# GpSimd's first two cache copies: 48 and 48 blocks on 16 engines become 24 and 72 blocks laid out eight wide

## What is computed

```python
def trunk_layer(x, start_pos, conv_buf, pool_buf, k_buf, v_buf, ...):
    h = rms_norm(x, norm_g)
    proj = jnp.einsum('btd,de->bte', h, w_in)
    ...
    kk = jnp.concatenate([k_buf, k], axis=1)
    vv = jnp.concatenate([v_buf, v], axis=1)
    o = dilated_attention(q, kk, vv, k_buf.shape[1])
    ...
    new_k = kk[:, -n_keep:]
    new_v = vv[:, -n_keep:]
    y = jnp.einsum('bte,ed->btd', jnp.concatenate([ya, yb, yc], axis=-1), w_out)
    return x + y, new_conv, new_pool, new_k, new_v
```

## Time and profile before

| | |
|---|---|
| median of 3 runs | 399.57 us (398.87 to 400.03) |
| profiled execution's own time | 398.96 us |
| span of its trace | 397.1 us |
| TensorE busy | 343.2 us (86%) |
| bytes moved by the 16 DMA engines | 157.73 MB, mean 397 GB/s |
| granted TensorE clock, mean | 0.946 |

### The profile page before, as it was taken

The page is one execution under the profiler, slowest core; times in us unless marked ns, Lnnn a source line. Parts: engine busy times, 40 slices in busy tenths (PEclk is TensorE's granted clock), DMA queues, the critical chain, the costliest instruction groups (busy, mean ns, idle before and its releaser), DMA issues.

```text
span 397.1 us, 4745 instructions
## 1 busy us (share of the span) xinstructions
PE 343.2 (86%) x1550; PEld 270.0 (68%) x1550; DVE 232.3 (58%) x530; ACT 100.1 (25%) x237; POOL 58.5 (15%) x110
## 2 busy tenths in 40 slices
PE   3897799998879859989958999999979867989990
PEld 2676578886557646578847888888747644658880
DVE  2603769759975996431013489978985997540110
ACT  4300013542523122411011011453352222230011
POOL 4007740003400011044001320000600002000000
PEclk9999989999969898999996999999978998989997
DMA  8999999999999999999999999999999999999982
GB/s 300 422 414 402 419 417 403 419 421 414 420 419 417 420 415 401 409 413 416 411 404 415 417 418 409 421 421 417 421 419 417 416 386 355 376 396 384 389 346 87
DMA packets 44329, 157.73 MB, mean 397 GB/s; under 512 B 6988, under 2 KB 20116, under 8 KB 44306
## 3 DMA queue, kind: packets, MB, share of 16 engines
q0 software_dynamic: 14624, 88.25, 54.5%
q10 hardware_dynamic: 14420, 41.52, 26.4%
q1 hardware_dynamic: 15262, 27.67, 18.7%
HBM read 140.23 MB, written 104.46 MB: 616 GB/s over the span
## 4 chain that ended last, share of the span: by engine, by line
PE 50%; DVE 14%; SPq 12%; DMA 10%; issue 5%; ACTq 4%; ACT 4%; DVEq 0%
PE pj L704 24%; PE pj L847 14%; SPq L491 11%; DMA kg<-in_cache_k_win 10%; DVE yc L1307 3%; PE psc L776 3%; PE ptr L622 3%; DVE ssc L1251 2%; ACTq L471 1%; PE ps L824 1%; ACTq L885 1%; DVE spsum_pad L1277 1%; DVE tok L1245 1%; DVE sc L1213 1%; PE ps L830 1%
## 5 line engine op out<-in xcount | busy, mean ns | idle before, releaser
L704 PE MATMUL pj<-hT,wt 128*128 128x264 f32 x800 | 195.5, 403 | 7.4 <-DVE hT L1162 5.0
L704 PEld LDWEIGHTS pj<-hT,wt 128*128 128x128 f32 x800 | 157.0, 200 | 39.7 <-issue 12.7
L1307 DVE SCALAR_TENSOR_TENSOR yc<-u_ext,par,yc 128x256 f32<-128x256 f32 x180 | 77.2, 480 | 3.8 <-DVE u_smp L1191 1.0
L847 PE MATMUL pj<-mix,wt 128*128 128x264 f32 x256 | 61.1, 395 | 0.0
L847 PEld LDWEIGHTS pj<-mix,wt 128*128 128x128 f32 x256 | 49.2, 195 | 8.4
L611 POOL DMA_DIRECT2D out<-in_cache_v_win x48 | 26.2, 553 | 143.3 <-issue 143.3
L1377 DVE TENSOR_TENSOR xT<-xT,pj 128x264 f32<-128x264 f32 x16 | 6.9, 430 | 55.2 <-PE pj L847 55.2
L611 POOL DMA_DIRECT2D out<-in_cache_k_win x48 | 26.4, 557 | 82.0 <-issue 82.0
L965 ACT ACTIVATE ex<-pj 128x264 f32<-128x264 f32 x22 | 8.6, 390 | 77.1 <-PE pj L704 44.0
L1245 DVE TENSOR_TENSOR tok<-kg,qb 128x1536 f32<-128x1536 f32 x10 | 17.6, 1758 | 4.2 <-DMA kg<-in_cache_k_win 3.7
L1189 DVE SCALAR_TENSOR_TENSOR u_ext<-ex,pj 128x256 f32<-128x256 f32 x6 | 2.5, 421 | 29.9 <-ACT ex L965 29.9
(11 more groups left out here) (187 smaller groups left out, 334.8 us busy)
## 6 DMA issues: line engine op xcount, KB each, us to landing
wt<-in_w_tiles ACTq DMA_DIRECT2D x62, 512.0 KB, 32.3
out<-in_cache_k_win POOLq DMA_DIRECT2D x24, 1080.0 KB, 44.4
out<-in_cache_v_win POOLq DMA_DIRECT2D x24, 1080.0 KB, 81.3
out<-in_cache_k_win POOLq DMA_DIRECT2D x8, 1200.0 KB, 72.0
out<-in_cache_v_win POOLq DMA_DIRECT2D x8, 1200.0 KB, 89.3
out<-in_cache_k_win POOLq DMA_DIRECT2D x16, 432.0 KB, 64.2
out<-in_cache_v_win POOLq DMA_DIRECT2D x16, 432.0 KB, 87.3
kg<-in_cache_k_win SPq DMA_DIRECT2D x32, 144.0 KB, 33.5
```

Source lines behind the costliest of these rows:

```text
L704: last = nc.tensor.matmul(pj[n % RING][:, 0:T], wt[:, g % WRING, k, :], hT[:, k, :], start=(k == 0), stop=(k == KD - 1))
L847: last = nc.tensor.matmul(pj[n % RING][:, 0:T], wt[:, g % WRING, k, :], mix[:, k, :], start=(k == 0), stop=(k == KD - 1))
L1307: last = V.scalar_tensor_tensor(out=yc[:, t, 0:SEQ], in0=x_w, scalar=par[:, ROW_CW + w * CT + t:ROW_CW + w * CT + t + 1], in1=yc[:, t, 0:S ...
```

## The change

In layer 1, kind "k", sample 0, the border between the first two copies moves from row 768 to row 384: 24 blocks and 72 blocks in place of 48 and 48. Line 605 lays these two out as 8 groups (of 3 and of 9 blocks) in place of 16 groups of 3. Rows, bytes, pieces, the number of copies, their order and their semaphores stay; every other copy is unchanged.

```diff
+HALVES_CUT = 8 * 3 * DEEP_STEP
+
+
+def engines_of(l, kind, s, a):
+
+    return 8 if (l, kind, s) == (DEPTH - 1, "k", 0) and a < FAR_LO else 16
+
+
+def main_zones(l, kind, s):
+
+    if engines_of(l, kind, s, 0) == 8:
+        return (0, HALVES_CUT), (HALVES_CUT, FAR_LO)
+    return ((0, FAR_LO // 2), (FAR_LO // 2, FAR_LO)) if (kind, l) in DEEP else ((0, EVEN_CUT), (EVEN_CUT, EVEN_ROWS))
+
+
 def copies_of(l):
 
     return [(kind, s, a, b) for kind in ("k", "v") for s in range(NS)
-            for a, b in (*(((0, FAR_LO // 2), (FAR_LO // 2, FAR_LO)) if (kind, l) in DEEP else ((0, EVEN_CUT), (EVEN_CUT, EVEN_ROWS))),
-                         (FAR_LO, GATHER[0][0]))]
+            for a, b in (*main_zones(l, kind, s), (FAR_LO, GATHER[0][0]))]
...
                     elif (kind, l) in DEEP:
-                        dst, src = (t.rearrange("(c e f) h d -> c e (f h d)", c=16, f=DEEP_STEP)[:, :, 0:(DEEP_STEP - 1) * C_ATT]
+                        dst, src = (t.rearrange("(c e f) h d -> c e (f h d)", c=engines_of(l, kind, s, a), f=DEEP_STEP)[:, :, 0:(DEEP_STEP - 1) * C_ATT]
                                     for t in (out[l, s, a:b], cache[l, s, a + 1:b + 1]))
```

## The result

The changed kernel took 400.7 us (median of 7 runs, 399.92 to 401.87), the one before 399.07 us (median of 7 in the same session, 398.06 to 400.03): ratio 1.0044, 95% interval 1.0025 to 1.0062, so 0.44% slower. Predicted were 401.3 us and +0.44%. The traced execution took 401.87 us, the longest of the seven and 1.2 us above their median; the traced one before took 398.96 us, close to its own. In what follows a block is one of 23,040 bytes, and a change of the time is always the ratio to the kernel before in the same session; 0.1% is 0.4 us.

A forecast was written before the change was run, and what follows sets the result against it. The prediction took one late DMA engine to bound the kernel: two more blocks at 0.89 us add 1.8 us, so 398.96 + 1.8 = 400.7 us for the profiled execution and 399.57 + 1.8 = 401.3 us (+0.44%) for a median; range 398.4 to 402.5.

The forecast's parts named there:

- The straggler bounds the kernel: At the end, one DMA engine works alone for the last 3.9 us to 396.2; its end plus 0.9 us is the span.
- the first eight: The eight engines on which an eight-row transfer lies; the engine that ends last was said to be one of them.
- Twelve engines: The 24 and 72 blocks each lie on twelve engines, giving eight engines 8 blocks instead of 6; chance 0.69.
- +1.8 us: Added time on the last-ending engine: two more blocks at 0.89 us each.
- Carried along to the end: The early delay stays in POOL's queue on the last-ending engine, which runs dry near 394 in place of 392.3.
- Weights and gathers not held back, computation unmoved: Engines take a packet of each queue in turn, so added packets delay only POOL's later copies, not weights and gathers.
- single-engine stretch: At the end, the DMA share falls to 0.06 at about the old time and stays there some 2 us longer.
- Same count of POOL packets: In the trace after, POOL's queue has the same number of packets and bytes as before.
- Eight engines a copy, in turn or the same eight: Rivals on the two copies: different eights, -1.3 us, chance 0.13; both on the same eight, +5.3 us, chance 0.04.
- Nothing shows: Rival: copies still dealt over about 16 engines, or the early backlog absorbed in idle time; 399.6 us, chance 0.11.
- The new wait in the middle: Rival: uneven POOL queue delays POOL's issue and state stores that layer 1's loads need; at most 1 us, no own chance.
- a lighter first eight: Small copy on the eight engines that include the last-ending one, 3 blocks instead of 6: 1.3 us gained, chance 0.13.

The follow-up runs named there:

- run 10: Kernel before with layer 1's first pair cut 40/56 in samples 0 and 1, each behind its own tiny two-piece POOL transfer: 398.75 us, ratio 0.9989.
- run 4: Kernel before with the first pair cut 40/56 behind a tiny POOL transfer of 8 rows of 256 B: 401.21 us, ratio 1.0050.
- run 1: Kernel before with the first pair (kind k, sample 0) cut into 40 and 56 blocks, no tiny transfer: 401.47 us, ratio 1.0051.
- run 12: Kernel before with only layer 1's last pair (kind v, sample 7) cut into 72 and 24 blocks: 394.91 us, ratio 0.9883.
- run 2: Kernel before with the first pair cut into 32 and 64 blocks, so every engine keeps 6: 399.64 us, ratio 1.0003.
- run 3: Kernel before with the kind k pairs of samples 0 and 1 cut 40/56, no tiny transfer: 401.02 us, ratio 1.0025.
- run 5: Kernel before with the first pair cut 40/56 behind a tiny POOL transfer of 8 rows of two 128 B pieces: 396.98 us, ratio 0.9949.
- run 7: Kernel before with samples 0 and 1 cut 40/56, the tiny POOL transfer ahead of the second pair: 403.6 us, ratio 1.0117.
- run 9: Kernel before with the first pair cut into 72 and 24 blocks behind the tiny POOL transfer: 396.11 us, ratio 0.9918.
- run 11: Kernel before with only layer 1's last pair (kind v, sample 7) cut into 40 and 56 blocks: 396.73 us, ratio 0.9931.
- run 6: Kernel before with 48 and 48 blocks kept and only the tiny POOL transfer added ahead of them: 399.17 us, ratio 1.0004.
- run 8: Kernel before with the first pair cut into 24 and 72 blocks behind the tiny POOL transfer: 400.03 us, ratio 1.0021.

## Why the prediction was right

**The straggler bounds the kernel: shown.** By the blocks on engines 4 to 6 against before: -4 gave 0.9918 and 0.9883 (and only 0.9989 in run 10, where the upper eight got 4 more), -2 gave 0.9949 and 0.9931, 0 gave 1.0003 and 1.0004, +2 gave 1.0044 and 1.0051 (and 1.0050 in run 4), +4 gave 1.0117. The time follows the blocks of a few engines, up and down, while the bytes in all are the same. Where the computation ends doesn't account for it: the spans of runs 1 and 12 are 7.0 us apart (400.1 and 393.1), SP's last issues only 0.7 us (389.81 and 389.07).

That the last engine is one of the first eight shows in every trace but that of run 12: the engine that moves the last of the eight 4 KB rows of `y_sample` is the one that ends last. This row moves 3.5 us behind the seventh in the kernel before (394.73 against 391.19), 3.2 us in the changed one, 6.1 us in run 1 and 1.2 us in run 12. One reading of the prediction was wrong without harm: SP's 18 packets in the last 3.9 us weren't shared out long before. They are mostly 2 KB rows of the result, issued from 388.40 on; the last engine is still busy with older work when they come, and they queue behind it.

**Twelve engines: shown by count.** +96 packets, with instructions that carry 24 and 72; and 40 and 56 blocks over ten and fourteen give 6 x 12 + 2 x 12 = 96, as counted. That the first eight carry the 8 blocks, from a start at engine 0 that moves on, rests on runs 1 to 5, which turn the sign by moving the start.

**+1.8 us: right.** 0.44% of 399.5 us is 1.8 (interval 1.0 to 2.5). The price of a block, which I took as 0.89 us from the mean of sixteen engines, is on the low side for this engine: the ratios of runs 1, 5, 7, 9, 11 and 12 give 1.0, 1.0, 1.2, 0.8, 1.4 and 1.2 us a block. Why the straggler pays more than the mean in most of them is open.

**Carried along to the end: shown.** The last data packet of POOL's queue ended at 392.25 us before, and at 392.41 and 392.85 with the usual blocks (runs 2 and 6); with two more on the last engine at 395.71 (the change), 396.48 and 396.50 (runs 1 and 4), with four more at 398.43; with two fewer at 390.03 and 390.19, with four fewer at 389.46 and 388.46 (runs 9 and 12). Runs 3, 8 and 10 fit less well, with 393.36, 394.71 and 392.44. A pair issued at 2 us and one issued near 102 us both move the end, the late one by no less (0.9931 against 0.9949, intervals that overlap). The size was off: 3.5 us later in the changed kernel, where I had said 394, 1.8 us later. Why this queue is late by more than its own added work isn't shown.

**Weights and gathers not held back, computation unmoved: not borne out by the profiled execution,** in which computation ended 2.7 us later. The control, run 2, shows the same long issue without any added block and the same time as before, and in runs 1, 2 and 6 the computation ended 0.6 us later, 0.6 us later and 1.4 us earlier without a matching shift of the end; so nothing speaks for a part of it in the 0.44%. The forecast of a single-engine stretch that starts at the old time and is 2 us longer failed for this reason: it started 2.7 us later (395.0 against 392.3) and was 0.3 us longer. In run 1, with the same load on the first eight, it came out. At 386 to 388 the share rose, as I said it would, but to 0.85, more than the blocks alone explain.

**Same count of POOL packets: wrong,** 96 more; bytes and pieces with data are the same.

**The rivals.** Eight engines a copy, in turn or the same eight, would have added 288 small packets; neither happened. "Nothing shows" is out by the interval. The new wait in the middle exists (6.55 us), but in the control too. The way that I had for the gain, a lighter first eight, is real: run 5 gave -2.0 us for two blocks less.

**Open:** runs 3 and 8, in which engines 4 to 6 end with their usual number of blocks but others don't, were 0.2% slower (both intervals lie above 1); why run 10's four blocks less brought only 0.7 us at the end; which single engine it is, since the numbers rest on the rule; and why this engine is the last one at all.

## What to carry to other kernels

When sixteen DMA engines work for one end, read the DMA share of the last microseconds in sixteenths: a tail at 0.06 is one engine, and a transfer's price is then what it puts on that engine, not its share of the bytes. Where the blocks are equally spaced, their number decides on how many engines a POOL copy lies, whatever groups the program writes, and the transfers ahead of it decide on which; so one constant made this kernel 0.5% slower (run 1) or 1.2% faster (run 12). Turn the suspected dose around before you believe in it: the gain found here was the predicted loss with its sign changed.

## What was unexpected in the hardware

A transfer of POOL that has one counting dimension (8 rows of 256 B) left the starting engine where it was (1.0050, as without it at 1.0051), one with two (8 rows of two 128 B pieces) moved it on (0.9949). Both move 2 KB from the same rows; the traces have 8 elements of 256 B for the one and 2 by 8 of 128 B for the other. The Trainium skill, "DMA: Bandwidth & Descriptors", section "Why a DMA increments its semaphore by 16 and not by 1", mentions that on this chip some direct copies of POOL's are spread over all sixteen instead. That would explain run 4, and the pair of runs 4 and 5 agrees with it.

An engine of the first eight ends last in the kernel before, the changed one and runs 1 to 11, and moving blocks on or off engines 4 to 6 moved the time in eight kernels. Its lag isn't chance. And ScalarE's issue of two stores, mostly 1.24 us, takes 3.3 to 6.6 us at the border of the layers in every kernel, with the sixteen DMA engines fully busy (share 1.03 before and 1.02 after the change, in the time of the issue); what it waits for there the traces don't show.
